# A fourth feature pair by seven products in the w_down stages, with the extra banks laid and kept by ScalarE

## The reference, cut to what matters

```
u = rms_norm(h, g_pre_mlp)                       # 256 x 2048
f = jnp.square(jax.nn.relu(u @ w_up)) @ w_down   # w_up 2048 x 8192, w_down 8192 x 2048
h = h + rms_norm(f, g_post_mlp)
```

## Time and profile before

| what | value |
|---|---|
| median of 3 runs | 2031.98 us |
| the profiled execution | 2031.48 us, span 2029.7 us |
| granted TensorE clock | 0.999 of full |
| TensorE busy | 2017.8 us, 99% of the span |
| VectorE busy | 1489.5 us, 73% |
| ScalarE busy | 985.2 us, 49% |
| DMA | mean 192 GB/s |

### The profile page before, as it was taken

One profiled execution on the slowest core, in us unless ns is written; L12 is line 12 of the kernel. 1 busy time (PEld: TensorE's weight loads), 2 busy tenths in 40 slices (PEclk: granted clock), 3 DMA queues, 4 the chain that ended last, 5 costly groups with the idle time before them and its releaser, 6 DMA issues.

```text
span 2029.7 us, 28875 instructions
## 1 busy us (share of the span) xinstructions
PE 2017.8 (99%) x10509; PEld 1719.2 (85%) x10509; DVE 1489.5 (73%) x2016; ACT 985.2 (49%) x1275; POOL 83.0 (4%) x91
## 2 busy tenths in 40 slices
PE   9999999999999999999999999999999999999998
PEld 7888898888888888999888888888888888888886
DVE  6766766566756655578999856587877887788887
ACT  6645444565544544433444644554553453354343
POOL 0000102001002000002000000000000000000001
PEclk9999999999999999999999999999999999999999
DMA  9688655655667665555666566655576466467554
GB/s 346 198 202 185 177 157 174 187 175 173 185 198 245 185 196 179 175 177 160 189 198 199 177 219 185 192 166 174 185 236 188 158 206 217 155 207 227 187 198 134
DMA packets 265475, 389.32 MB, mean 192 GB/s; under 512 B 12504, under 2 KB 147032, under 8 KB 264571
## 3 DMA queue, kind: packets, MB, share of 16 engines
q1 hardware_dynamic: 262587, 377.19, 60.9%
q0 software_dynamic: 2624, 10.54, 1.9%
q10 hardware_dynamic: 144, 0.01, 0.0%
HBM read 385.02 MB, written 2.54 MB: 191 GB/s over the span
## 4 chain that ended last, share of the span: by engine, by line
PE 98%; SPq 1%; DMA 1%; DVE 0%; ACT 0%; issue 0%; DVEq 0%
PE acc L701 18%; PE acc L678 17%; PE acc L680 17%; PE acc L679 17%; PE acc L699 10%; PE acc L692 2%; PE acc L691 2%; PE acc L693 2%; PE acc L697 1%; PE aux L730 1%; PE aux L732 1%; PE aux L731 1%; PE acc L730 1%; PE acc L731 1%; PE acc L732 1%; PE aux L1619 1%
## 5 line engine op out<-in xcount | busy, mean ns | idle before, releaser
L532 DVE TENSOR_TENSOR low_rows<-stage_rows,high_rows 128x1024 fp32r<-128x1024 f32 x480 | 575.2, 1210 | 295.6 <-ACT high_rows L518 286.9
L518 ACT ACTIVATE high_rows<-stage_rows 128x1024 fp32r<-128x1024 f32 x480 | 495.5, 1040 | 542.2 <-PE acc L680 480.8
L518 ACT ACTIVATE w_high<-stage 128x1024 fp32r<-128x1024 f32 (+1 forms) x264 | 276.1, 1047 | 405.1 <-PE acc L701 298.0
L532 DVE TENSOR_TENSOR w_low<-stage,w_high 128x1024 fp32r<-128x1024 f32 (+1 forms) x264 | 319.8, 1221 | 176.1 <-ACT w_high L518 171.5
L701 PE MATMUL acc<-u,w_high 128*128 128x512 f32 x900 | 247.9, 394 | 0.0
L701 PE MATMUL acc<-hT,w_high 128*128 128x512 f32 x645 | 177.5, 394 | 0.0
L701 PEld LDWEIGHTS acc<-u,w_high 128*128 128x128 f32 x900 | 152.9, 189 | 19.0
L699 PEld LDWEIGHTS acc<-u,w_low 128*128 128x128 f32 x960 | 146.8, 188 | 20.5
L699 PE MATMUL acc<-u,w_low 128*128 128x256 f32 x960 | 152.5, 281 | 0.0
L678 PE MATMUL acc<-high_rows,hT 128*128 128x512 f32 x384 | 151.8, 395 | 0.0
L680 PE MATMUL acc<-high_rows,hT 128*128 128x512 f32 x384 | 149.6, 390 | 0.0
(11 more groups left out here) (451 smaller groups left out, 3601.4 us busy)
## 6 DMA issues: line engine op xcount, KB each, us to landing
stage_rows<-in_w_in SPq DMA_DIRECT2D x160, 512.0 KB, 3.8
stage<-in_w_in SPq DMA_DIRECT2D x136, 512.0 KB, 3.6
stage_rows<-in_w_down SPq DMA_DIRECT2D x128, 512.0 KB, 4.4
stage<-in_w_up SPq DMA_DIRECT2D x120, 512.0 KB, 4.5
stage_rows<-in_w_o SPq DMA_DIRECT2D x64, 512.0 KB, 4.1
stage_rows<-in_w_pool_out SPq DMA_DIRECT2D x16, 512.0 KB, 3.9
stage_rows<-in_w_conv_out SPq DMA_DIRECT2D x16, 512.0 KB, 4.4
stage_rows<-in_w_mem_kv SPq DMA_DIRECT2D x14, 512.0 KB, 11.2
```

The costliest lines, as they stand in the source:

```text
L518: act.activation(high[:, pr, k_from:kt, 0:p.cols], src[:, slot, k_from:kt, 0:p.cols], ACT.Copy).then_inc(high_done, 1)
L532: dve.tensor_tensor(low[:, pr, k_from:kt, 0:p.cols], src[:, slot, k_from:kt, 0:p.cols], high[:, pr, k_from:kt, 0:p.cols].bitcast(F32), ALU ...
```

## The change

SEVENS becomes (2, 3, 5, 6): four couples in a step, S = 24, in the order 4 plain slabs, couple, couple, 2 plain, couple, couple, 2 plain. Where a couple follows another one directly, its OUTER sum is made before the split of the first couple's INNER slab and its INNER sums before the split of its own LEFT slab, two slabs sooner than else. There are four sets of feature sums, the fourth in a place of its own. The z banks are no longer added by VectorE: ScalarE keeps them after each of the seven steps (copy to z_rows: banks 0 and 1 in the hook of the last INNER slab, 2 and 3 in that of the slab behind it) and lays the sum so far back into the banks before the next couple of the same columns (five steps, 20 copies; in the hooks of slabs 4 and 5 of w_up{q}, or of slabs 0 and 1 of the second step). TensorE's first product on a laid bank accumulates instead of starting anew. The spreading waits for the last keeping.

```
-SEVENS = (2, 4, 6)
+SEVENS = (2, 3, 5, 6)
...
-        f_sums = at("f_sums", Z + 32, [P, len(SEVENS), 2, 4, P], F32R)
+        sums_at = [(Z + 32 + 4 * e, Z + 34 + 4 * e) for e in range(3)] + [(74.25, 82.75)]
+        f_sums = [[at(f"f_sums{e}{half}", kb, [P, 4, P], F32R) for half, kb in enumerate(places)] for e, places in enumerate(sums_at)]
...
-                        SUMS_BEFORE.update({n + 1: (OUTER, n), n + 2: (INNER, n)})
+                        ahead = 2 if job.kinds[idx - 1] == INNER else 0
+                        SUMS_BEFORE.update({n + 1 - ahead: (OUTER, n), n + 2 - ahead: (INNER, n)})
...
-                if e == 0 and step:
-                    if step <= 2:
-                        pe.wait_ge(s("z_copied"), 4 * step)
-                    else:
-                        pe.wait_ge(s("z_summed"), 4 * (step - 2))
+                if e == 0 and step == 1:
+                    pe.wait_ge(s("z_copied"), 4)
+                elif e == 0 and step:
+                    pe.wait_ge(s("z_laid"), 4 * (step - 1))
...
-                pe.matmul(bk, x_high, high, start=own and e == 0, stop=False)
+                laid = own and step >= 2
+                pe.matmul(bk, x_high, high, start=own and e == 0 and not laid, stop=False, skip_group_check=laid)
...
-                    act.wait_ge(s("z_summed"), 21)
+                    act.wait_ge(s("z_spread"), 1)
...
-            def copy_z(q):
+            def lay_z(q, step, banks):
+
+                act.wait_ge(s("z_copied"), 4 * (2 * q + step))
+                for b in banks:
+                    act.activation(aux[:, b, :], z_rows[step][b][:], ACT.Copy).then_inc(s("z_laid"), 1)
+
+            def keep_z(q):
...
+                    if q and step and idx < 2:
+                        lay_z(q, step, (2 * idx, 2 * idx + 1))
-                    for b in {inner: (0, 1), inner + 2: (2, 3)}.get(idx, ()):
+                    for b in {inner: (0, 1), inner + 1: (2, 3)}.get(idx, ()):
...
+            def lay_first(q):
+
+                def beside(n):
+                    if n in (4, 5):
+                        lay_z(q, 0, (2 * n - 8, 2 * n - 7))
+                return beside
+
             for q in range(4):
-                rounding(f"w_up{q}", beside=beside_up0 if q == 0 else None)
-                rounding(f"w_down{q}", beside=copy_z(q) if q == 0 else None)
+                rounding(f"w_up{q}", beside=lay_first(q) if q else beside_up0)
+                rounding(f"w_down{q}", beside=keep_z(q))
...
-            def sum_z(q):
...
-                        dve.tensor_tensor(v[:], aux[:, b, :], v[:], ALU.add).then_inc(s("z_summed"), 1)
...
-                    dve.wait_ge(s("z_summed"), 16 if step else 20)
+                    dve.wait_ge(s("z_copied"), 24 if step else 28)
...
-                splitting(f"w_down{q}", down_body(q, f"w_down{q}"), beside=sum_z(q) if q else None, at_once=True)
+                splitting(f"w_down{q}", down_body(q, f"w_down{q}"), at_once=True)
```

More of the change, by code:

```diff
@@ L722, in seven_products @@
             x4 = [p.rows[:, k0 + 1, half, P:2 * P] for half in range(2)]
-            sums = [[f_sums[:, e, half, r, :] for half in range(2)] for r in range(4)]
+            sums = [[f_sums[e][half][:, r, :] for half in range(2)] for r in range(4)]
             products = {LEFT: [(0, x1, aux[:, 0, :], True), (1, x2, acc[:, 2 * one, :], False)],
@@ L729, in seven_products @@
                 high, low = high_rows[:, pr, k, :], low_rows[:, pr, k, :]
-                pe.matmul(bk, x_high, high, start=own and e == 0, stop=False)
-                pe.matmul(bk, x_high, low, start=False, stop=False)
-                mm = pe.matmul(bk, x_low, high, start=False, stop=own and e == len(SEVENS) - 1)
+                laid = own and step >= 2
+                pe.matmul(bk, x_high, high, start=own and e == 0 and not laid, stop=False, skip_group_check=laid)
+                pe.matmul(bk, x_high, low, start=False, stop=False, skip_group_check=laid)
+                mm = pe.matmul(bk, x_low, high, start=False, stop=own and e == len(SEVENS) - 1, skip_group_check=laid)
             mm.then_inc(used, 1)
@@ L2578, in feature_sums @@
                 link(dve.tensor_tensor(f_raw[:, 3, :], f[:, 2, :], f_raw[:, 2, :], ALU.subtract))
-                link(dve.tensor_copy(f_sums[:, e, 0], f_raw[:]))
-                dve.tensor_tensor(f_sums[:, e, 1], f_raw[:], f_sums[:, e, 0].bitcast(F32), ALU.subtract).then_inc(s("f_sums_ready"), 1)
+                link(dve.tensor_copy(f_sums[e][0][:], f_raw[:]))
+                dve.tensor_tensor(f_sums[e][1][:], f_raw[:], f_sums[e][0][:].bitcast(F32), ALU.subtract).then_inc(s("f_sums_ready"), 1)
             def down_body(q, name, first=0):
@@ L2616, in z_spread @@
                     link(dve.tensor_tensor(y22, y22, z5[:], ALU.subtract))
-            def sum_z(q):
[L2619 to L2631, removed]
-                        dve.tensor_tensor(v[:], aux[:, b, :], v[:], ALU.add).then_inc(s("z_summed"), 1)
-                return beside
             def spread(name, step, n):
                 if n in SPREAD_AT[name]:
-                    dve.wait_ge(s("z_summed"), 16 if step else 20)
+                    dve.wait_ge(s("z_copied"), 24 if step else 28)
                     z_spread(step, SPREAD_AT[name].index(n))
@@ L2642, in beside_last @@
                 if n == SPREAD_AT["w_down_last"][-1]:
-                    dve.sem_inc(s("z_summed"), 1)
+                    dve.sem_inc(s("z_spread"), 1)
             def last_down():
```

## The result

The changed kernel takes 2035.02 us (median of 17 runs, 2034.21 to 2036.25) against 2031.25 us (median of 17, 2030.34 to 2032.21): ratio 1.0019, 95% interval 1.0012 to 1.0025, 3.8 us slower. The forecast was 3.4 us slower (8.2 - 4.76). Its profiled execution has a span of 2033.2 us, 3.5 more than before.

The account below looks back on a forecast made before the run. TensorE, busy 99% of the span, was taken as the bound: profiled 2031.48 - 4.76 for matmuls removed + 8.2 of waits = 2034.9 us, 2035.4 for the median; 8-in-10 range 2027.0 to 2039.5.

Parts of the forecast that it names:

- What goes: TensorE in w_down: 28 couples instead of 21 remove 21 matmuls of 0.2268 us, all on the chain, -4.76 us.
- Average load of VectorE fits: VectorE per w_down step: demand rises from 36.4 of 41.5 us to 38.3 of 40.8 us, still fitting on average.
- The chain at a site: Where a couple directly follows another: from first LEFT product (T0), second LEFT ready at 5.35 us, not 4.76: 0.59 us waiting.
- Seven steps, two sites each alike: w_down, pairs 3 and 6 of each step: both sites cost the same, 7 x 2 x 0.59 = +8.2 us.
- Everything else at nothing: ScalarE's 40 more bank copies, four more feature sums in w_up, DMA and the kernel's end add no time.
- Cover holds: Rival: TensorE nowhere waits and the full 4.76 us are gained, 2027.2 us; chance 0.13.
- Falls further behind: Rival: VectorE later at second couple's OUTER and INNER splits, 0.6 us more per site, +12 us, 2044; chance 0.14.
- Late banks or slabs: Rival: laid banks or slab landings late at some of 14 places, 0.5 to 1 us each, about 2040; chance 0.05.
- The rule on the drain: VectorE's site chain: next instruction starts only with pipeline empty; first half gives 0.75 us per site, +10.5 us, 2037.7; rejected.

Follow-up runs that it names:

- the first experiment: Changed kernel with SEVENS = (2, 4, 6), so no couple directly follows another, banks still kept and laid: 2031.57 us against 2031.51 for the kernel before, ratio 1.0001.
- the reordered kernels: Changed kernel with three plain slabs ahead of either two couples: 2037.93 us; the same with both second couples' sums one slab sooner: 2032.26 us; kernel before 2031.96.

## Why the prediction was right, step by step

- *What goes*, 4.76 us: shown. 21 instructions fewer on TensorE, and the kernel with one addition left out is 5.1 us under the kernel before, with no wait in the way.
- *Average load of VectorE fits*: shown. It is busy 38.1 us of 42.01 in a step (forecast demand 38.3), and taking load off elsewhere gains nothing.
- *The chain at a site*, 0.59 us: measured 0.58, with the four starts from INNER's split on within 0.01 us. One reading of the prediction was wrong and cost nothing: it took the start of the new OUTER sum from the second site (forecast +0.21, measured +0.18 there) for both. At the first site that sum starts at -0.23, and 0.37 us of VectorE are left behind it. What the chain's length rests on (where sums stand in the order) was tested by moving them both ways: 15.6 us lost, 4.2 us gained.
- *Seven steps, two sites each alike*: 14 waits, all 0.33 or 0.34 by their row. That both have one cause was only half right. At the first site VectorE has 1.4 us of gaps and only the order is at fault; at the second it is full from LEFT's split on, so moving the sums makes it worse (0.72). The two bounds happened to coincide at T0 + 1.36, which I had computed and not weighed. That the second site costs the same as the first is luck to that extent.
- *Everything else at nothing*: the banks by the first experiment; feature sums, since from one w_down to the next TensorE's first waits lie 1608.59 - 1434.85 = 173.74 us apart, two steps of 42.01 and 89.7 of w_up. In the kernel before, w_up1 takes 89.7 us too, from 1501.9, the end of the earlier trace rows's first stretch, to 1591.6.
- *The rivals.* "Cover holds" fell, for the reason given against it. "Falls further behind" didn't come here, but came in the reordered kernels, at a place that I hadn't named. "Late banks or slabs": no wait of that kind.
- *The rule on the drain* of the Trainium skill's page "VectorE: DVE Perf Modes" (section "The DRAIN you can't avoid") by its first half asked for 0.75 us per site. The measured 0.58, and starts 0.08 us ahead of the end (1647.86 behind 1646.71 + 1.23), decide for the second half.

## What to carry to other kernels

When an engine with spare time feeds the bound one through a ring of buffers, follow the loop from the release of a buffer to the product that needs it, start by start, and compare it with the bound engine's time for the same slabs: here 5.35 against 4.76 us, invisible in a load of 94% (38.3 of 40.8 us). Work for a later slab belongs in a gap of the feeder before that loop starts. Where the feeder had no gap (read the idle time in its timeline), moving the work only moved the wait. Look at what stands ahead of each group, evacuations above all, before an order is judged by its steady state.

## What the runs showed that I had not expected

A copy by ScalarE of 128x512 from z_rows into a bank (0.583 us) takes as long as one out of it (0.584). After a wait at the OUTER or INNER product the first matmul's row is 0.50 us and those behind it keep a slightly longer distance for some time (1663.42, 1663.66, 1663.89: 0.235 us instead of 0.227), which may add some hundredths to such a wait; behind LEFT of pair 3 the distance is 0.23 (1650.93, 1651.16).
